# One stage of rounds in place of a norm stage and a latent-projection stage, in a hybrid decoder step

## The chip, the cores and the metric

The kernel runs on one core of a Trainium2 chip. The metric is the device time of one execution, in microseconds (us). The core has five engines that take their instructions in order and hand work to each other by semaphores: PE (TensorE, matrix products and transposes into PSUM), ACT (ScalarE), DVE (VectorE), POOL (GpSimd) and SP (SyncE, which here issues most DMAs).

## The reference, cut to what matters

The reference is one layer of a decoder for a prompt of 2048 tokens and a sample group of 32 tokens (8 x 4). Everything starts with one norm and one wide projection:

```
xn = x * rsqrt(mean(x*x) + 1e-6) * g_pre                       # 2048 x 1024 and 32 x 1024
[qa | ka | va | za | cq | ckv | kpe | zb | ma | mb] = xn @ w_in
```

The change touches the norm and the columns cq (256), ckv (128) and kpe (32), 416 in all, the latents of the second attention branch:

```
cq_n  = rms_norm(cq, g_q)            # feeds the queries later on
ckv_n = rms_norm(ckv, g_kv)          # an output, and keys and values later on
kpe_r = kpe * cos + rot(kpe) * sin   # an output, and a key shared by all heads
```

All other columns, the attention branches, the gates and the output projection are worked out in later stages, which the change leaves as they are. Everything is float32; products are made from a high and a low part of each operand, three matmuls in place of one.

## The kernel before, in words

`run_stages` calls one stage after the other; a stage is one block of engine programs, and the next block begins when all engines and the stage's awaited stores are through. The first two stages are the subject.

`stage_norm` goes over 17 tiles (16 of 128 prompt tokens, one of 32 sample tokens), two at a time, in a loop over pairs (`peeled`). For a tile, SP loads 128 x 1024 of x (L160); ACT takes the sum of squares (L173) and a square root (L176); DVE inverts it (L200) and multiplies x by it and by the gains (L203); PE transposes the result in eight blocks of 128 x 128 into PSUM (L229); ACT copies that into `xT_hi` (L181), rounded to the matmul's format; DVE writes the rest into `xT_lo` (L208). `xT_hi` and `xT_lo` stay in SBUF for all later projections. Both tiles of a pair go through one step before ACT and DVE turn to the next step.

`stage_latents` first loads the 416 columns of `w_in` in eight chunks through two buffers (L276), with ACT making the high part (L306) and DVE the low part (L342); PE waits for all eight (`w_lo`). Then it goes over the same 17 tiles: PE makes 24 matmuls (8 chunks of the 1024 x 3 parts; L109, L110, L111 in `split_matmul`) into one of four PSUM banks; ACT takes two sums of squares, a copy and two roots (L323 to L331); DVE finishes the latents in `nat` (L350 to L364); SP stores ckv and kpe (L291, L292); PE transposes the tile's latents in four pieces (L376, L378), one tile later; ACT lays these out in `cqT`, `ckvT`, `kpeT` (L314 to L316), which hold all 2080 tokens. When the last tile is laid out, SP stores the three whole (L295 to L297) and waits for them.

The third stage, `stage_dilated`, begins with loads of its own weights (its tiles are named `dil_...`).

Of the kernel before, what the change touches and what calls it, by code (L numbers as in the profile page):

```python
# [26 lines left out]
F32 = mybir.dt.float32  # L27
# [5 lines left out]
ds = bass.ds  # L33
# [99 lines left out]


def stage_norm(nc, t, xT, xs, ident):

    with ExitStack() as ctx:
        m = Mem(nc, ctx, "norm")
        xin = [m.sb(f"xin{b}", [P, D]) for b in range(2)]
        xn = [m.sb(f"xn{b}", [P, D]) for b in range(2)]  # L140
        junk = m.sb("junk", [P, D])
        g = m.sb("g_rows", [P, D])
        eps = m.sb("eps", [P, 1])
        stat = [m.sb(f"stat{b}", [P, 4]) for b in range(2)]
        tp = [m.ps(f"tp{b}", [P, KC, P]) for b in range(2)]
        consts = m.sem("consts")
        x_in = [m.sem(f"x_in{b}") for b in range(2)]
        eps_set, squared, rooted, inverted = (m.sem(n) for n in ("eps_set", "squared", "rooted", "inverted"))
        xn_ready, tp_ready, hi_ready, lo_ready = (m.sem(n) for n in ("xn_ready", "tp_ready", "hi_ready", "lo_ready"))

        with nc.Block() as block:
            @block.sync
            def _(sp):
                sp.dma_start(ident[:, :], t["ident"]).then_inc(consts, 16)
                sp.dma_start(g[:, :], t["g_pre"].partition_broadcast(P)).then_inc(consts, 16)

                def load(i):
                    for b in range(2):
                        waits(sp, xn_ready, i + b - 1)
                        sp.dma_start(xin[b][:, :], t["x_prompt"][ds((i + b) * P, P), :]).then_inc(x_in[b], 16)  # L160

                peeled(sp, NT // 2, 2, load)
                sp.wait_ge(xn_ready, NT - 1)
                sp.dma_start(xin[0][0:NS, :], t["x_sample"]).then_inc(x_in[0], 16)

            @block.scalar
            def _(act):
                act.wait_ge(eps_set, 1)

                def square(n, b, loads, rows):  # L170
                    act.wait_ge(x_in[b], loads)
                    waits(act, inverted, n - 1)
                    act.activation(junk[0:rows, :], xin[b][0:rows, :], ACT.Square,  # L173
                                   accum_out=stat[b][0:rows, 0:1]).then_inc(squared, 1)
                    act.wait_ge(squared, n + 1)
                    act.activation(stat[b][0:rows, 1:2], stat[b][0:rows, 0:1], ACT.Sqrt, bias=eps[0:rows, :],  # L176
                                   scale=1.0 / D).then_inc(rooted, 1)

                def high(n, b, out, rows):
                    act.wait_ge(tp_ready, n + 1)  # L180
                    act.activation(out, tp[b][:, :, 0:rows], ACT.Copy).then_inc(hi_ready, 1)  # L181

                def pair(i):
                    for b in range(2):
                        square(i + b, b, i * 8 + 16, P)
                    for b in range(2):
                        high(i + b, b, xT[0][:, :, ds((i + b) * P, P)], P)

                peeled(act, NT // 2, 2, pair)
                square(NT, 0, NT * 8 + 16, NS)  # L190
                high(NT, 0, xs[0][:, :, :], NS)

            @block.vector
            def _(dve):
                dve.memset(eps[:, :], EPS).then_inc(eps_set, 1)
                dve.wait_ge(consts, 32)

                def norm(n, b, rows):
                    dve.wait_ge(rooted, n + 1)
                    dve.reciprocal(stat[b][0:rows, 2:3], stat[b][0:rows, 1:2]).then_inc(inverted, 1)  # L200
                    dve.wait_ge(inverted, n + 1)
                    waits(dve, tp_ready, n - 1)
                    dve.scalar_tensor_tensor(xn[b][0:rows, :], xin[b][0:rows, :], stat[b][0:rows, 2:3],  # L203
                                             g[0:rows, :], ALU.mult, ALU.mult).then_inc(xn_ready, 1)

                def low(n, b, hi, lo, rows):
                    dve.wait_ge(hi_ready, n + 1)
                    dve.tensor_tensor(lo, tp[b][:, :, 0:rows], hi.bitcast(F32), ALU.subtract).then_inc(lo_ready, 1)  # L208

                def pair(i):  # L210
                    for b in range(2):
                        norm(i + b, b, P)
                    for b in range(2):
                        at = ds((i + b) * P, P)
                        low(i + b, b, xT[0][:, :, at], xT[1][:, :, at], P)

                peeled(dve, NT // 2, 2, pair)
                norm(NT, 0, NS)
                low(NT, 0, xs[0][:, :, :], xs[1][:, :, :], NS)

            @block.tensor
            def _(pe):
                pe.wait_ge(consts, 32)

                def turn(n, b, rows):
                    pe.wait_ge(xn_ready, n + 1)
                    waits(pe, lo_ready, n - 1)
                    for c in range(KC):
                        last = pe.transpose(tp[b][:, c, 0:rows], xn[b][0:rows, c * P:(c + 1) * P],  # L229
                                            ident[0:rows, 0:rows])  # L230
                    last.then_inc(tp_ready, 1)

                def pair(i):
                    for b in range(2):
                        turn(i + b, b, P)

                peeled(pe, NT // 2, 2, pair)
                turn(NT, 0, NS)


def stage_latents(nc, t, xT, xs, ident):

    with ExitStack() as ctx:
        m = Mem(nc, ctx, "lat")
        raw = [m.sb(f"raw{b}", [P, LAT]) for b in range(2)]
        w = [m.sb(f"w_{h}", [P, KC, LAT], F32R) for h in ("hi", "lo")]
        lat = [m.sb(f"lat{b}", [P, LAT]) for b in range(2)]
        nat = [m.sb(f"nat{b}", [P, LAT]) for b in range(2)]
        rot = [m.sb(f"rot{b}", [P, 2 * ROPE]) for b in range(2)]
        junk_q, junk_kv = m.sb("junk_q", [P, QL]), m.sb("junk_kv", [P, KL])  # L250
        stat = [m.sb(f"stat{b}", [P, 6]) for b in range(2)]
        eps = m.sb("eps", [P, 1])
        gkv = m.sb("gkv_rows", [P, KL])
        gq = m.sb("gq_cols", [P, QL // P])
        cs = m.sb("rope_rows", [P, NT + 1, 2, ROPE])
        cqT = m.sb("cqT", [P, QL // P, TOK])
        ckvT = m.sb("ckvT", [P, TOK])
        kpeT = m.sb("kpeT", [ROPE, TOK])
        pj = [m.ps(f"pj{b}", [P, 512]) for b in range(4)]
# [2134 lines left out]
```

## Time and profile before

| | us |
|---|---|
| timed, median of 3 runs (3608.48 to 3610.82) | 3609.86 |
| the profiled execution's own time | 3615.65 |
| span of that execution, first to last instruction | 3614.1 |
| PE busy in the span | 3344.3 (93%) |
| DVE, ACT, POOL busy | 1314.3, 954.7, 443.8 |
| mean granted TensorE clock, share of full speed | 0.954 |

The span is divided by the profile into 40 slices of some 90 us; the two stages of the change fill the first two and a little of the third. A line of the timeline reads: start, duration, engine, line of the kernel, operation, what it writes <- what it reads, shapes, count, and in brackets how long the engine sat idle before it and what released it. SPq is SP's queue of DMA issues, PEld the weight loads of PE. A transpose is listed as MATMUL.

### The profile page before, as it was taken

The numbers are of one execution on the slowest core, as the hardware profiler recorded it, in microseconds if no ns is written. First come the engines' busy times: TensorE is split into PE (matmuls) and PEld (weight loads), VectorE is DVE, ScalarE is ACT, GpSimd is POOL, SyncE is SP. The second block draws the span as 40 slices with busy tenths as digits, with TensorE's granted clock in tenths as the row PEclk, the third lists the DMA queues.
The fourth block names the chain that finished last, engine by engine and source line by source line (L and its number), as shares of the span: only waits on it lengthen the run. The fifth ranks groups of instructions, "written<-read, shape, count | busy, mean of one in ns | idle before, by whom it ended". The sixth has DMA issues, their size and how long they took to land. (4 is left out here: it accounts for less than half of the span.)

```text
span 3614.1 us, 51439 instructions
## 1 busy us (share of the span) xinstructions
PE 3344.3 (93%) x19384; PEld 2785.8 (77%) x19384; DVE 1314.3 (36%) x3518; ACT 954.7 (26%) x1839; POOL 443.8 (12%) x599
## 2 busy tenths in 40 slices
PE   3979999999999999899999997899999999488799
PEld 3968888888788887799999996566666667288787
DVE  5202222222222222222111112466555666388433
ACT  5412222222222222122222222233333334110121
POOL 0000000000000000000000002223322312044200
PEclk6989999999999998899999999899999999699899
DMA  3143333333323332332222214133333223377343
GB/s 115 27 165 120 122 121 100 108 111 97 120 92 106 96 103 72 98 95 82 84 84 84 82 60 138 56 106 116 116 116 108 75 59 114 128 253 245 104 139 119
DMA packets 348182, 391.52 MB, mean 108 GB/s; under 512 B 111465, under 2 KB 305738, under 8 KB 345898
## 3 DMA queue, kind: packets, MB, share of 16 engines
q1 hardware_dynamic: 308474, 173.53, 17.5%
q0 software_dynamic: 39472, 214.82, 17.1%
q8 instruction: 150, 2.46, 0.3%
q14 instruction: 86, 0.70, 0.1%
HBM read 309.62 MB, written 166.67 MB: 132 GB/s over the span
## 5 line engine op out<-in xcount | busy, mean ns | idle before, releaser
L109 PE MATMUL dil_PJ<-all_xT_hi,dil_w_hi 128*128 128x512 f32 x1152 | 469.6, 408 | 17.6 <-DVE dil_w_lo L634 17.6
L111 PE MATMUL dil_PJ<-all_xT_hi,dil_w_lo 128*128 128x512 f32 x1152 | 454.7, 395 | 0.0
L110 PE MATMUL dil_PJ<-all_xT_lo,dil_w_hi 128*128 128x512 f32 x1152 | 454.6, 395 | 0.0
L109 PE MATMUL gate_ps<-all_xT_hi,gate_w_hi 128*128 128x416 f32 x960 | 346.1, 360 | 13.5 <-DVE gate_w_lo L1082 13.5
L111 PE MATMUL gate_ps<-all_xT_hi,gate_w_lo 128*128 128x416 f32 x960 | 337.7, 352 | 0.0
L110 PE MATMUL gate_ps<-all_xT_lo,gate_w_hi 128*128 128x416 f32 x960 | 337.0, 351 | 0.0
L1857 PE MATMUL mla_S<-mla_k,mla_q 96*128 96x512 f32 (+3 forms) x640 | 294.2, 578 | 12.7 <-ACT mla_p L1645 7.3
L109 PEld LDWEIGHTS dil_PJ<-all_xT_hi,dil_w_hi 128*128 128x128 f32 x1152 | 216.9, 188 | 98.9 <-issue 36.1
L1885 PE MATMUL mla_O<-mla_v,mla_pT 128*128 128x66 f32 x2176 | 272.8, 275 | 4.6 <-DVE mla_rec L1804 4.6
L1885 PEld LDWEIGHTS mla_O<-mla_v,mla_pT 128*128 128x128 f32 x2176 | 265.1, 196 | 9.0 <-issue 7.2
L111 PEld LDWEIGHTS dil_PJ<-all_xT_hi,dil_w_lo 128*128 128x128 f32 x1152 | 216.7, 188 | 50.1
L110 PEld LDWEIGHTS dil_PJ<-all_xT_lo,dil_w_hi 128*128 128x128 f32 x1152 | 217.1, 188 | 43.5
L668 DVE COPY dil_rec<-dil_O 128x256 f32<-128x256 f32 x96 | 40.8, 425 | 510.9 <-PE dil_O L791 510.9
L1789 DVE TENSOR_REDUCE mla_stat<-mla_S 128x1 f32<-128x1024 f32 (+2 forms) x192 | 175.0, 912 | 85.2 <-PE mla_S L1857 80.7
L579 ACT ACTIVATE dil_sm<-dil_sm,dil_neg 128x256 f32<-128x256 f32 (+1 forms) x384 | 146.1, 451 | 222.9 <-DVE dil_neg L655 222.9
L1645 ACT ACTIVATE mla_p<-mla_S,mla_stat 128x1024 f32<-128x1024 f32 (+2 forms) x192 | 166.1, 865 | 129.9 <-DVE mla_stat L1791 128.9
L648 DVE CUSTOM_DVE_ANT_0 dil_sm<-dil_S,dil_bias 128x256 f32<-128x256 f32 (+1 forms) x384 | 117.6, 362 | 215.9 <-PE dil_S L763 213.2
L109 PEld LDWEIGHTS gate_ps<-all_xT_hi,gate_w_hi 128*128 128x128 f32 x960 | 180.7, 188 | 18.7 <-DVE gate_w_lo L1082 13.7
L1857 PEld LDWEIGHTS mla_S<-mla_k,mla_q 96*128 96x128 f32 x640 | 111.9, 200 | 107.2 <-issue 79.6
L1653 ACT ACTIVATE mla_pT<-mla_T 128x512 f32<-128x512 f32 (+1 forms) x192 | 104.0, 542 | 325.0 <-PE mla_T L1867 324.1
L110 PEld LDWEIGHTS gate_ps<-all_xT_lo,gate_w_hi 128*128 128x128 f32 x960 | 181.4, 189 | 1.9
L111 PEld LDWEIGHTS gate_ps<-all_xT_hi,gate_w_lo 128*128 128x128 f32 x960 | 180.7, 188 | 2.4
(272 smaller groups left out, 5743.1 us busy)
## 6 DMA issues: line engine op xcount, KB each, us to landing
out_win_sample<-in_state_win POOLq DMA_DIRECT2D x16, 4088.0 KB, 15.2
mla_kv<-in_state_win POOLq DMA_DIRECT2D x72, 512.0 KB, 12.5
scr_gates<-gate_out POOLq DMA_DIRECT2D x120, 208.0 KB, 2.3
mla_qb<-scr_hs POOLq DMA_DIRECT2D x32, 768.0 KB, 12.2
dil_raw<-in_w_in SPq DMA_DIRECT2D x36, 512.0 KB, 4.3
gate_ckv<-in_cache_ckv SPq DMA_DIRECT2D x256, 64.0 KB, 1.8
out_win_sample<-in_state_win POOLq DMA_DIRECT2D x8, 2032.0 KB, 8.6
jp_gm<-scr_gates SPq DMA_DIRECT2D x56, 256.0 KB, 4.8
```

The costliest lines, as they stand in the source:

```text
L109: pe.matmul(out, w[0], x[0], start=first, stop=False)
L110: pe.matmul(out, w[0], x[1], start=False, stop=False)
L111: return pe.matmul(out, w[1], x[0], start=False, stop=last)
L579: last = act.activation(part, part, ACT.Exp, bias=neg[u % 2][:, s, h:h + 1])
L648: last = dve.tensor_tensor_reduce(sm[:, s, h, 0:nk * P], S[:, h, s * 2 * P:(s * 2 + nk) * P], bias[:, h, (2 - nk) * P:2 * P], 1.0, LOWEST, ...
L668: dve.tensor_copy(rec[u % 4][:, :, 0:2 * HD], O[:, :, 2:2 + 2 * HD])
L1645: act.activation(p[u % 2][:, 0:nk * P], s2[:, 0:nk * P], ACT.Exp, bias=stat[u % 2][:, 1:2], scale=B_SCALE).then_inc(exped, 1)
L1653: act.activation(pT[u % 2][0][:, 0:q, :], T[:, 0, 0:q, :], ACT.Copy).then_inc(t_out_a, 1)
L1789: dve.tensor_reduce(stat[b2][:, 0:1], s2[:, 0:nk * P], AX.X, ALU.max).then_inc(maxed, 1)
L1857: last = pe.matmul(S[:, 2 * (u % 2) + a // 4, 0:width], q96[0:NOPE + ROPE, i * P:(i + 1) * P], k96[0:NOPE + ROPE, (j + a) * P:(j + a) * P ...
L1885: last = pe.matmul(O[:, u % 2, 0:VB], pT[u % 2][k // 4][:, k % 4, :], v[:, j + k, :], start=k == 0, stop=k == nk - 1)
```

## The change: one stage, in rounds

`stage_norm` and `stage_latents` are taken out, and `stage_norm_and_latents` does both. It runs 21 rounds with no loop instruction; round i squares and normalises tile i, turns it (PE), makes the high part and the low part and the projection of tile i-1, takes the projected latents of tile i-2, transposes the latents of tile i-3 and lays out those of tile i-4. The weights are loaded and split inside round 0. The projection has two PSUM banks in place of four (`pj`), since the turned x keeps four (`xp`). `cqT`, `ckvT` and `kpeT` hold one tile each, twice, and each tile of them is stored on its own.

```diff
+def stage_norm_and_latents(nc, t, xT, xs, ident):
...
+        cqT = [m.sb(f"cqT{b}", [P, QL // P, P]) for b in range(2)]
+        ckvT = [m.sb(f"ckvT{b}", [P, P]) for b in range(2)]
+        kpeT = [m.sb(f"kpeT{b}", [ROPE, P]) for b in range(2)]
+        xp = [m.ps(f"xp{b}", [P, KC, P]) for b in range(2)]
+        pj = [m.ps(f"pj{b}", [P, 512]) for b in range(2)]
+        tp = [m.ps(f"tp{b}", [P, 4, P]) for b in range(2)]
...
+        TILES = NT + 1
+        ROUNDS = TILES + 4
...
+                def load_x(i):
+                    if i > 1:
+                        sp.wait_ge(xn_ready, i - 1)
...
+                def load_weights(c):
+                    if c > 1:
+                        sp.wait_ge(w_lo, c - 1)
+                    sp.dma_start(raw[c % 2][:, :], t["w_in"][c * P:(c + 1) * P, C_CQ:C_CQ + LAT]).then_inc(w_in[c % 2], 16)
+
+                load_x(0)
+                sp.dma_start(ident[:, :], t["ident"]).then_inc(x_consts, 16)
+                sp.dma_start(g[:, :], t["g_pre"].partition_broadcast(P)).then_inc(x_consts, 16)
+                load_x(1)
+                load_weights(0)
+                load_weights(1)
+                sp.dma_start(gkv[:, :], t["g_kv"].partition_broadcast(P)).then_inc(consts, 16)
...
+                def store_turned(i):
+                    sp.wait_ge(turned, i + 1)
+                    cols = slice(0, rows_of(i))
+                    sp.dma_start(t["cqT"][:, :, at(i)].rearrange("c p n -> p c n"), cqT[i % 2][:, :, cols])\
+                        .then_inc(t_stored[i % 2], 16)
+                    sp.dma_start(t["ckvT"][:, at(i)], ckvT[i % 2][:, cols]).then_inc(t_stored[i % 2], 16)
+                    sp.dma_start(t["kpeT"][:, at(i)], kpeT[i % 2][:, cols]).then_inc(t_stored[i % 2], 16)
...
+                for i in range(ROUNDS):
+                    if i + 2 < TILES:
+                        load_x(i + 2)
+                    if i == 0:
+                        for c in range(2, KC):
+                            load_weights(c)
+                    if 0 <= i - 2 < TILES:
+                        store_latents(i - 2)
+                    if 0 <= i - 4 < TILES:
+                        store_turned(i - 4)
...
+                def lay_out(i):
+                    b, n = i % 2, rows_of(i)
+                    act.wait_ge(tp_ready, i + 1)
+                    if i > 1:
+                        act.wait_ge(t_stored[b], 48 * (i // 2))
...
+                for i in range(ROUNDS):
+                    if i < TILES:
+                        square(i)
+                    if 0 <= i - 1 < TILES:
+                        high(i - 1)
+                    if i == 0:
+                        for c in range(KC):
+                            high_weight(c)
+                        act.wait_ge(consts, 64)
+                    if 0 <= i - 2 < TILES:
+                        take(i - 2)
+                    if 0 <= i - 4 < TILES:
+                        lay_out(i - 4)
...
+                for i in range(ROUNDS):
+                    if i < TILES:
+                        norm(i)
+                    if 0 <= i - 1 < TILES:
+                        low(i - 1)
+                    if i == 0:
+                        for c in range(KC):
+                            low_weight(c)
+                        dve.wait_ge(consts, 64)
+                    if 0 <= i - 2 < TILES:
+                        finish(i - 2)
...
+                def project(i):
+                    pe.wait_ge(lo_ready, i + 1)
+                    if i == 0:
+                        pe.wait_ge(w_lo, KC)
+                    if i > 1:
+                        pe.wait_ge(copied, i - 1)
+                        pe.wait_ge(squared, 2 * (i - 1))
...
+                for i in range(ROUNDS):
+                    if i < TILES:
+                        turn_x(i)
+                    if 0 <= i - 1 < TILES:
+                        project(i - 1)
+                    if 0 <= i - 3 < TILES:
+                        turn_latents(i - 3)
...
-        stage_norm(nc, t, xT, xs, ident)
-        stage_latents(nc, t, xT, xs, ident)
+        stage_norm_and_latents(nc, t, xT, xs, ident)
```

The functions `square`, `high`, `high_weight`, `take`, `lay_out` (ACT), `norm`, `low`, `low_weight`, `finish` (DVE), `turn_x`, `project`, `turn_latents` (PE) issue the same compute instructions, on tiles of the same sizes, as the lines of before that the section on the kernel names.

PE, between one projection and the next. Before, in `stage_latents` (`lat_pj` is the projection, `lat_tp` the transposed latents):

```order
L111 MATMUL lat_pj<-lat_w_hi,all_xT_lo 128x416
L376 MATMUL lat_tp<-all_ident,lat_nat 128x128 x3
L378 MATMUL lat_tp<-all_ident,lat_nat 32x128
L109 MATMUL lat_pj<-lat_w_hi,all_xT_hi 128x416
L110 MATMUL lat_pj<-lat_w_lo,all_xT_hi 128x416
```

PE at the same place in a middle round of the change (`nl_xp` is the turned x):

```order
L111 MATMUL nl_pj<-nl_w_hi,all_xT_lo 128x416
L2268 MATMUL nl_tp<-all_ident,nl_nat 128x128 x3
L2269 MATMUL nl_tp<-all_ident,nl_nat 32x128
L2245 MATMUL nl_xp<-all_ident,nl_xn 128x128 x8
L109 MATMUL nl_pj<-nl_w_hi,all_xT_hi 128x416
L110 MATMUL nl_pj<-nl_w_lo,all_xT_hi 128x416
```

Between two projections there now stand the eight transposes of a later tile of x, which before were in the first stage.

ACT, one tile of `stage_latents` before:

```order
L323 ACTIVATE lat_junk_q,lat_stat<-lat_pj 128x256
L325 ACTIVATE lat_junk_kv,lat_stat<-lat_pj 128x128
L327 ACTIVATE lat_lat<-lat_pj 128x416
L329 ACTIVATE lat_stat<-lat_stat,lat_eps 128x1
L331 ACTIVATE lat_stat<-lat_stat,lat_eps 128x1
L314 ACTIVATE lat_cqT<-lat_tp,lat_gq_cols 128x128 x2
L315 ACTIVATE lat_ckvT<-lat_tp 128x128
L316 ACTIVATE lat_kpeT<-lat_tp 32x128
```

ACT, one middle round of the change (`nl_xin` is x as loaded, `nl_xstat` its statistics):

```order
L2123 ACTIVATE nl_junk,nl_xstat<-nl_xin 128x1024
L2125 ACTIVATE nl_xstat<-nl_xstat,nl_eps 128x1
L2131 ACTIVATE all_xT_hi<-nl_xp 128x8x128
L2142 ACTIVATE nl_junk,nl_stat<-nl_pj 128x256
L2143 ACTIVATE nl_junk,nl_stat<-nl_pj 128x128
L2145 ACTIVATE nl_lat<-nl_pj 128x416
L2147 ACTIVATE nl_stat<-nl_stat,nl_eps 128x1
L2149 ACTIVATE nl_stat<-nl_stat,nl_eps 128x1
L2158 ACTIVATE nl_cqT<-nl_tp,nl_gq_cols 128x128 x2
L2159 ACTIVATE nl_ckvT<-nl_tp 128x128
L2160 ACTIVATE nl_kpeT<-nl_tp 32x128
```

Three instructions of the first stage now come ahead of the second stage's eight in each round, and the copy into `xT_hi` stands between a root and a projected tile.

SP's queue at the end of the stage before:

```order
L291 DMA out_ckv_sample<-lat_nat 32x128
L292 DMA out_kpe_sample<-lat_nat 32x32
L295 DMA scr_cqT<-lat_cqT 128x2080 x2
L296 DMA scr_ckvT<-lat_ckvT 128x2080
L297 DMA scr_kpeT<-lat_kpeT 32x2080
```

SP's queue at the end of the new stage:

```order
L2088 DMA out_ckv_sample<-nl_nat 32x128
L2089 DMA out_kpe_sample<-nl_nat 32x32
L2094 DMA scr_cqT<-nl_cqT 128x2x128
L2096 DMA scr_ckvT<-nl_ckvT 128x128
L2097 DMA scr_kpeT<-nl_kpeT 32x128
L2094 DMA scr_cqT<-nl_cqT 128x2x128
L2096 DMA scr_ckvT<-nl_ckvT 128x128
L2097 DMA scr_kpeT<-nl_kpeT 32x128
L2094 DMA scr_cqT<-nl_cqT 128x2x32
L2096 DMA scr_ckvT<-nl_ckvT 128x32
L2097 DMA scr_kpeT<-nl_kpeT 32x32
```

The four whole stores have become three small ones for each tile; the stores of the last three turned tiles stand behind those of the last latents.

## Rows read from the trace of the kernel before

**Rows 1.** Busy time by stretch: PE, PEld, DVE, ACT, POOL, granted clock, DMA share, GB/s
```profile
12.50:79.00 66.50, 30.40 (x136) 27.12 (x136) 43.80 (x50) 38.02 (x65) 0.00 (x0) 0.67 0.37 112
...
102.00:170.00 68.00, 68.00 (x385) 66.73 (x384) 14.73 (x98) 31.34 (x150) 0.00 (x0) 1.00 0.07 18
...
21.60:25.30 3.70, 3.67 (x16) 3.28 (x16) 1.68 (x2) 1.02 (x1) 0.00 (x0) 1.00 0.60 178
```

**Rows 2.** Timeline of the kernel's start
```profile
1.00 0.40 SPq L154 DMA_DIRECT2D all_ident<-in_ident  x1
...
8.01 1.28 ACT L173 ACT_TABLE_LOAD   x1 [8.01 <-DMA norm_xin<-in_x_prompt]
...
12.37 1.28 DVE L203 SCALAR_TENSOR_TENSOR norm_xn<-norm_xin,norm_stat,norm_g_rows 128x1024 f32<-128x1024 f32 x1
```

**Rows 3.** Timeline of one pair of tiles in the norm stage
```profile
26.35 1.05 ACT L173 ACTIVATE norm_junk<-norm_xin 128x1024 f32<-128x1024 f32 x1
...
27.52 0.29 ACT L176 ACTIVATE norm_stat<-norm_stat,norm_eps 128x1 f32<-128x1 f32 x1
...
27.85 0.16 DVE L200 RECIPROCAL norm_stat<-norm_stat 128x1 f32<-128x1 f32 x1
28.13 1.28 DVE L203 SCALAR_TENSOR_TENSOR norm_xn<-norm_xin,norm_stat,norm_g_rows 128x1024 f32<-128x1024 f32 x1
...
29.55 3.67 PE L229 MATMUL norm_tp<-all_ident,norm_xn 128*128 128x128 f32 x16 [4.25 <-DVE norm_xn L203]
...
31.65 1.02 ACT L181 ACTIVATE all_xT_hi<-norm_tp 128x1024 f32 x1 [2.47 <-PE norm_tp L229]
32.82 1.22 DVE L208 TENSOR_TENSOR all_xT_lo<-norm_tp,all_xT_hi 128x1024 f32 x1 [2.01 <-ACT all_xT_hi L181]
```

**Rows 4.** Timeline of the weights, to the first projection
```profile
81.52 1.09 ACT L306 ACTIVATE lat_w_hi<-lat_raw 128x416 fp32r<-128x416 f32 x2 [3.15 <-DMA lat_raw<-in_w_in]
82.10 1.13 DVE L342 TENSOR_TENSOR lat_w_lo<-lat_raw,lat_w_hi 128x416 fp32r<-128x416 f32 x2 [2.87 <-ACT lat_w_hi L306]
...
94.67 0.71 PE L109 MATMUL lat_pj<-lat_w_hi,all_xT_hi 128*128 128x416 f32 x1 [16.73 <-DVE lat_w_lo L342]
```

**Rows 5.** Timeline of PE where its matmuls become shorter
```profile
99.69 0.55 PE L111 MATMUL lat_pj<-lat_w_hi,all_xT_lo 128*128 128x416 f32 x1
100.04 0.52 PE L109 MATMUL lat_pj<-lat_w_hi,all_xT_hi 128*128 128x416 f32 x1
```

**Rows 6.** Timeline of one latent tile: PE, then ACT, then DVE
```profile
106.44 0.49 PE L376 MATMUL lat_tp<-all_ident,lat_nat 128*128 128x128 f32 x3
...
106.79 0.43 PE L109 MATMUL lat_pj<-lat_w_hi,all_xT_hi 128*128 128x416 f32 x1
...
111.39 0.49 PE L376 MATMUL lat_tp<-all_ident,lat_nat 128*128 128x128 f32 x3
...
111.59 0.38 ACT L323 ACTIVATE lat_junk_q<-lat_pj 128x256 f32<-128x256 f32 x1 [2.66 <-PE lat_pj L111]
...
112.98 0.63 ACT L314 ACTIVATE lat_cqT<-lat_tp,lat_gq_cols 128x128 f32<-128x128 f32 x2
...
113.64 0.25 ACT L316 ACTIVATE lat_kpeT<-lat_tp 32x128 f32<-32x128 f32 x1
...
114.00 0.18 DVE L364 TENSOR_TENSOR lat_nat<-lat_rot 128x32 f32<-128x32 f32 x1
```

**Rows 7.** Timeline of the latent stage's end and the next stage's first instruction
```profile
180.92 0.37 ACT L323 ACTIVATE lat_junk_q<-lat_pj 32x256 f32<-32x256 f32 x1 [2.64 <-PE lat_pj L111]
...
184.59 0.82 SPq L295 DMA_DIRECT2D scr_cqT<-lat_cqT  x2
...
195.05 0.13 POOL L542 MEMSET dil_v<- 128x16 f32 x1 [194.35 <-POOLq L271]
```

**Rows 8.** DMA issues of the two stages: count, KB each, median us to landing
```profile
norm_xin<-in_x_prompt SPq DMA_DIRECT2D x16, 512.0 KB, 4.2
...
scr_ckvT<-lat_ckvT SPq DMA_DIRECT2D x1, 1040.0 KB, 8.1
...
out_kpe_sample<-lat_nat SPq DMA_DIRECT2D x1, 4.0 KB, 1.6
```

More of the change, by code:

```diff
@@ L132, in peeled @@
         body(i * step)
[L135 to L238, printed above, removed]
```

299 lines of the change are left out of this document (158 added, 141 removed).

## The prediction

> **What bounds the kernel now.** I read the busy time by stretch first, then the timeline of each stretch. Only the kernel's first 195 us are touched, and there no engine is full until the projections run. In the norm stage, 66.5 us hold 30.4 us of PE, 43.8 of DVE and 38.0 of ACT [rows 1]: three engines take turns, since within a pair PE waits for the normalised tiles (4.25 us idle before its 16 transposes), ACT for PE, DVE for ACT [rows 3]. Then comes a stretch with nothing but weights: PE's first projection starts at 94.67 and has waited 16.73 us for the last remainder [rows 4]. From 102 to 170 PE is busy all the time at a granted clock of 1.00, with ACT under half and DVE under a quarter busy [rows 1]: that stage is bound by PE. At its end the last tile is taken at 180.92, SP begins the four large stores at 184.59, and the next stage's first instruction is at 195.05 [rows 7]; the stores alone cost 10.5 us with every engine idle.
>
> So the first two stages are worth 195.05 us, of which PE needs 17 times 4.95 [rows 6], 84, for the projections. The question is how far a round is from PE's own work.
>
> **The change part by part.**
>
> *A round on PE.* One latent tile takes 4.95 us from transposes to transposes (106.44 to 111.39): 0.35 for the four pieces, 4.60 for 24 matmuls, a pitch of 0.19 [rows 6]. The round adds eight transposes. Sixteen took 3.67 in the norm stage, 0.23 each [rows 3]; the same shape inside the projections takes about 0.11 (three full pieces and one narrow one in 0.35) [rows 6]. The first is the pace at the clock's lower level, 1.2 GHz, the second at 2.4. PE works without a pause in the rounds, as from 102 to 170, so I take 0.11: 0.9 us. A round is 0.9 + 4.95 = 5.85, with one more switch of shape 5.9. The other end is 0.23, 1.84 us for eight and 6.8 a round.
>
> *Does the rest of the round fit under it?* ACT: square and root 1.46 (26.35 to 27.81), high part 1.02 [rows 3], take 1.39 (111.59 to 112.98), lay out 0.91 (to 113.89) [rows 6]: 4.8. DVE: inverse and product 1.56 (27.85 to 29.41), low part 1.22 [rows 3], finishing at most 1.20 (112.98 to 114.18) [rows 6]: 4.0. Both are under 5.9, but what counts is the chain through them. After a projection ends, ACT takes it (1.39), lays out an older tile (0.91), squares a new one (1.46); DVE normalises that (1.56) and then makes the low part that the next projection but one waits for (1.22): 6.54, and five hand-overs of 0.04 (root to inverse, 27.81 to 27.85) to 0.15 (high to low, 32.67 to 32.82) [rows 3], 6.7 to 7.3. PE meanwhile has 0.35 + 0.9 + 4.6 + 0.35 + 0.9 = 7.1. So the chain just fits; at the slow end it costs 0.2 in every second round, 2 us in all. I take nothing. The high part (1.02) runs beside DVE's 1.56.
>
> *Memory traffic in a round.* The x load is issued when a tile is normalised and is needed two rounds less 3 us later, 8.7 us; it lands in 4.2 [rows 8]. The three turned stores wait on SP behind two latents stores, and `lay_out` waits for those of two tiles before: cover 11.8 - 0.9, need three issues of 0.41 [rows 7] and a landing between 1.6 and 8.1 [rows 8], 9.3 at worst. Cost nothing; without that cover a late landing would hold ACT and through it every projection. SP is free for 48 more issues.
>
> *The start.* x comes first in SP's queue, not third: landed at 1.00 + 4.2 = 5.2 in place of 8.01 [rows 2, 8]. Tile 0 was normalised 5.64 after its landing (8.01 to 13.65, with a table load at its head) [rows 2], now at 10.85. By then the first two weight chunks, two issues behind the second x tile, should have landed, but DVE's first remainder stands behind that product. From first remainder to first projection took 12.57 (82.10 to 94.67) [rows 4], four pairs each waiting for the one before; the change keeps two buffers, so the weights are split at 23.4, and 0.5 later as an x tile and the rope rows queue ahead: 23.9 (bounds: 22 if x lands at once, 27 if it lands at 8.01 as before). ACT, 0.6 earlier, squares tile 1 to 24.8; DVE normalises to 26.3, makes the low part of tile 0 to 27.7; PE turns tile 1 from 26.4 at the lower clock (1.84) and projects tile 0 from 28.2. Before, that was 94.67.
>
> *The rounds.* Before, PE ran at the long pitch of 0.35 from 94.67 to 100.04 [rows 4, 5], 5.4 us after a long idle; here from 26.4 to 31.8. Ten matmuls at 0.35 and 14 at 0.19 end projection 0 at 34.5. Projections 1 and 2 have no latents to turn: 5.5 each, 45.5. Thirteen rounds of 5.9: 122.2. The last has no x to turn: 4.95, 127.2.
>
> *The tail.* From take to finished latents 2.6 (111.59 to 114.18) [rows 6]: 129.8. SP issues two stores, then only the three of tile 14, 0.41 each: the last is issued at 131.4 and lands 1.6 later [rows 8], 133.0; ACT's lay-out of tile 16 waits for them, 0.91, 133.9; three more issues and a landing: 136.4. Small stores stand between 1.6 and the 8.1 of the 1040 KB store [rows 8]; the new ones are 128 KB at most, so 1.6, and two landings at 8.1 would add 13.
>
> *Sum.* The next stage starts at 136.4 in place of 195.05: 58.6, I take 58. Everything behind it moves up as it is. The profiled span of 3614.1 becomes 3556. That execution took 3615.65 in all, the timed median is 3609.86, so the timed kernel comes to 3609.86 - 58 = 3552.
>
> **The rivals.**
>
> *Forecast: PE-bound rounds.* 3552, own range 3546 to 3560: start 2 us earlier or 3 later, hand-overs 2, tail to half its bound. Chance 0.69.
>
> *The chain bounds the rounds.* It fits by 0.4 us at the fast hand-over only. If queued work or late semaphores make it 8.5, two rounds take 1.4 more, a round is 6.6 and thirteen of them cost 9: 3561. For it: the slack is small. Against it: in unrolled code the hand-overs are 0.04. Chance 0.15.
>
> *The transposes are slow at either clock.* From 21.60 to 25.30 the granted clock reads 1.00 while 16 transposes still take 3.67 [rows 1]. If that reading is right, 0.23 is their price whatever the clock, rounds are 6.8, and fifteen of them cost 14: 3566. Against: the same duration in the pair of rows 3, which belongs to a stretch of mean clock 0.67 that must hold lower readings, and 0.11 in rows 6 for the same shape. Chance 0.08.
>
> *The clock swings.* PE now waits for another engine at three places in each round, and `pj` has two banks in place of four. If its clock fell in each round to the mean 0.67 of the norm stage [rows 1], a round is 5.9 / 0.67 = 8.8 and sixteen cost 46: 3598, still faster by 0.3%. Against: the norm stage had PE idle more than half of the time, the rounds have waits of tenths of a microsecond. Chance 0.05. The Trainium skill, in "TensorE: Matmul & The Clock Gate", section "A second HAM failure mode: psum-queue depth-cycling", speaks for this rival: a kernel that cycled through PSUM banks paused briefly between groups often enough for its clock to go back and forth. By that rule the time would be this rival's, by the stretch from 102 to 170, where `pj` cycles too and the clock stays at 1.00, it would be the forecast; no row yet shows two banks.
>
> *The other side: PE stays at the lower clock through the whole stage.* Matmuls at 0.35 and transposes at 0.23 make a round 8.4 + 1.84 + 0.7 = 10.9, five more, sixteen times 80: 3632, slower by 0.6%. It decides from a round of 5.9 + 58/16 = 9.5 on. Against: at that pace PE has no waits at all, and without waits the clock rose within 5.4 us [rows 4, 5]. Chance 0.03.
>
> **How the numbers follow.** About 0.2%, 7 us, is what a measurement can tell from no change. Forecast, chain, transposes and swinging clock are all faster by more: 0.69 + 0.15 + 0.08 + 0.05 = 0.97, of which I move 0.01 to no change for a swing somewhat deeper than the norm stage's; slower 0.03. The range reaches from the forecast's lower end to beyond the slow transposes with a start 3 us late and a slow hand-over: 3546 to 3572, which leaves out the two clock cases and a little of the others, 1 to 2 in 10.
>
> **What would show it.** In the changed profile: the first projection at about 28 and the 17th ending at about 127; a pitch of 5.9 between transposes of x, PE without idle time and a clock of 1.00 from about 32 on; eight transposes in 0.9; `lay_out` of the last tile released by a store, and the next stage's first instruction near 136. Wrong would be: PE idle before `turn_x` released by DVE in most rounds (chain), eight transposes in 1.8 at full clock, a clock below 1.00 in the rounds, or ACT released by `scr_cqT` stores before the tail.

## The result, and the profile after

| | change, us | before, us | ratio, 95% interval |
|---|---|---|---|
| first timing, median (lowest to highest, runs) | 3556.16 (3547.63 to 3559.12, 4) | 3609.17 (3601.70 to 3610.82, 4) | 0.9850, 0.9834 to 0.9866 |
| second timing | 3551.50 (3547.66 to 3557.50, 5) | 3605.77 (3602.07 to 3618.02, 9) | 0.9844, 0.9824 to 0.9864 |
| profiled execution: span | 3556.7 | 3614.1 | |
| first instruction of the next stage | 136.55 | 195.05 [rows 7] | |

The kernel became 53.0 and 54.3 us faster; the forecast said 58 and 3552. The two stages themselves gave up 195.05 - 136.55 = 58.5 us. The profile after, place by place, against the rows ahead of the prediction:

The timeline of the start (columns as before: start, duration, engine, line, operation, and in brackets the idle time and its releaser) answers to [rows 2, 4, 5]:

```profile
4.78 1.28 ACT L2123 ACT_TABLE_LOAD   x1 [4.78 <-DMA nl_xin<-in_x_prompt]
...
9.14 1.28 DVE L2189 SCALAR_TENSOR_TENSOR nl_xn<-nl_xin,nl_xstat,nl_g_rows 128x1024 f32<-128x1024 f32 x1
...
22.36 1.06 ACT L2135 ACTIVATE nl_w_hi<-nl_raw 128x416 fp32r<-128x416 f32 x2 [2.62 <-DMA nl_raw<-in_w_in]
22.94 1.10 DVE L2199 TENSOR_TENSOR nl_w_lo<-nl_raw,nl_w_hi 128x416 fp32r<-128x416 f32 x2 [2.58 <-ACT nl_w_hi L2135]
...
26.43 1.97 PE L2245 MATMUL nl_xp<-all_ident,nl_xn 128*128 128x128 f32 x8 [13.92 <-DVE nl_xn L2189]
...
28.05 0.69 PE L109 MATMUL nl_pj<-nl_w_hi,all_xT_hi 128*128 128x416 f32 x1
...
28.54 0.55 PE L110 MATMUL nl_pj<-nl_w_lo,all_xT_hi 128*128 128x416 f32 x1
...
28.89 0.55 PE L111 MATMUL nl_pj<-nl_w_hi,all_xT_lo 128*128 128x416 f32 x1
...
32.33 0.35 PE L109 MATMUL nl_pj<-nl_w_hi,all_xT_hi 128*128 128x416 f32 x1
...
32.52 0.35 PE L110 MATMUL nl_pj<-nl_w_lo,all_xT_hi 128*128 128x416 f32 x1
```

x is there at 4.78, tile 0 is normalised at 10.42, the weights are split at 24.04, the first projection starts at 28.05, where before it was 94.67. The weights still come in pairs that ACT waits for, 2.62 us at the last, and PE sits idle for 13.92 us. From start to start the projection's matmuls first stand 0.35 us apart (28.54, 28.89) and from 32.33 on 0.19.

A middle round, on the timeline, answers to [rows 6]:

```profile
63.61 1.04 PE L2245 MATMUL nl_xp<-all_ident,nl_xn 128*128 128x128 f32 x8
64.40 0.44 PE L109 MATMUL nl_pj<-nl_w_hi,all_xT_hi 128*128 128x416 f32 x1
...
69.06 0.49 PE L2268 MATMUL nl_tp<-all_ident,nl_nat 128*128 128x128 f32 x3
...
69.26 0.39 ACT L2142 ACTIVATE nl_junk<-nl_pj 128x256 f32<-128x256 f32 x1 [1.31 <-PE nl_pj L111]
...
69.49 1.04 PE L2245 MATMUL nl_xp<-all_ident,nl_xn 128*128 128x128 f32 x8
...
74.35 1.22 DVE L2195 TENSOR_TENSOR all_xT_lo<-nl_xp,all_xT_hi 128x1024 fp32r<-128x1024 f32 x1
...
76.17 0.44 PE L109 MATMUL nl_pj<-nl_w_hi,all_xT_hi 128*128 128x416 f32 x1
```

From transposes to transposes it is 69.49 - 63.61 = 5.88 us. Eight transposes hold PE for 64.40 - 63.61 = 0.79 to the start of the next matmul, and the 24 matmuls behind them take 69.06 - 64.40 = 4.66, 0.19 each. ACT waits 1.31 us for PE's projection: PE is the engine that sets the pace. The low part made from tile to tile ends at 74.35 + 1.22 = 75.57, and the projection that reads it starts at 76.17, so 0.60 us of slack are left in that chain.

Busy time in the rounds (columns as in [rows 1]), then the longest of the waits in the rounds, 60 to 120 (engine, line <- releaser: us in total, times, longest):

```profile
60.00:125.00 65.00, 65.00 (x396) 62.34 (x395) 37.88 (x109) 47.79 (x162) 0.00 (x0) 1.00 0.36 110
```

```profile
ACT nl_junk L2142 <- PE nl_pj L111: 13.1, 10, 1.3
```

PE is busy in all of the 65 us at a granted clock of 1.00, the upper level of 2.4 GHz; it waits for nobody, ACT waits for it once in each of ten rounds, and no wait of PE, ACT or DVE is ended by a DMA.

The end of the stage, on the timeline, answers to [rows 7]:

```profile
126.90 0.49 PE L2268 MATMUL nl_tp<-all_ident,nl_nat 128*128 128x128 f32 x3
...
129.48 0.17 DVE L2220 TENSOR_TENSOR nl_nat<-nl_rot 32x32 f32<-32x32 f32 x1
...
131.50 0.44 SPq L2097 DMA_DIRECT2D scr_kpeT<-nl_kpeT  x1
...
133.08 0.47 ACT L2158 ACTIVATE nl_cqT<-nl_tp,nl_gq_cols 128x32 f32<-128x32 f32 x2 [2.88 <-DMA scr_kpeT<-nl_kpeT]
...
134.64 0.43 SPq L2097 DMA_DIRECT2D scr_kpeT<-nl_kpeT  x1
136.55 0.13 POOL L284 MEMSET dil_v<- 128x16 f32 x1 [135.85 <-POOLq L2056]
```

The last lay-out waits 2.88 us for a store that SP issued at 131.50, and that lands 1.6 later; 1.9 us after the last issue, at 134.64, the next stage starts. From the end of the last projection, where the transposes of 126.90 start, to the next stage it is 136.55 - 126.90 = 9.65 us.

**Why 53 and 54 and not 58.5.** Behind the first instruction of the next stage, the program is the same. From there to the end of the span, eleven profiled executions (before, the change twice, eight experiments) took 3409.9 to 3420.2 us: 3614.1 - 195.05 = 3419.1 before, 3556.7 - 136.55 = 3420.2 and 3549.6 - 136.98 = 3412.6 in two executions of the change. One and the same kernel differs there by 7.6 us.

The first instruction of POOL in the stage of the second attention branch, late in that rest, parts it in two. Its line before, then in the change:

```profile
2216.39 0.44 POOL L1581 MEMSET mla_spz<- 128x416 f32 x1 [5.15 <-POOLq L2299]
```

```profile
2160.61 0.44 POOL L1323 MEMSET mla_spz<- 128x416 f32 x1 [5.09 <-POOLq L2313]
```

The change's other execution has it at 2161.10, so 55.8 and 55.3 of the 58.5 are left there. The way from the next stage's first instruction to it takes 2021.3 us before, 2024.1 in both executions of the change and 2020.7 to 2024.7 in the experiments; whether the 2.8 given back belong to the change stays open at that spread. From there to the end the eleven executions take 1387.7 to 1397.7, and this last part holds most of their differences: of the change's two executions, the longer has 1396.1 there at a mean granted clock over the span of 0.962, the shorter 1388.5 at 0.964. Why it differs is open. The experiments below are therefore read by the end of the stage, where the change's two executions agree to 0.43 us, and not by the whole time.

### The profile page after: what moved, and what is told of

Same layout as the page of the kernel before. It is cut to its first block and busy times, and to the rows that moved or that the text cites. A ratio compares the mean times of both kernels' runs of the same rounds, so it can differ in the third digit from the quotient of the medians.

```text
span 3556.7 us, 51335 instructions
## 1 busy us (share of the span) xinstructions
PE 3331.7 (94%) x19384; PEld 2776.4 (78%) x19384; DVE 1312.5 (37%) x3517; ACT 952.7 (27%) x1839; POOL 444.0 (12%) x599
## 3 DMA queue, kind: packets, MB, share of 16 engines
q0 software_dynamic: 39472, 214.82, 17.4%
```

## The experiments

Each line says where the next stage's first instruction came; before it is 195.05, in the change 136.55. The first six were timed in one execution each (3607.59, 3587.85, 3558.70, 3589.84, 3552.81 and 3549.20 us, in their order here), the last two in five.

**1. Only the stores, in the old order.** The kernel before, with the turned latents stored tile by tile.

```diff
-        cqT = m.sb("cqT", [P, QL // P, TOK])
+        cqT = [m.sb(f"cqT{b}", [P, QL // P, P]) for b in range(2)]
...
-                for c in range(QL // P):
-                    sp.dma_start(t["cqT"][c], cqT[:, c, :]).then_inc(stored, 16)
...
+                    if i:
+                        store_turned(i - 1, P)
+                store_turned(NT, NS)
...
+                    waits(act, t_stored[b], 48 * (i // 2))
```

> The kernel before with one part of the change alone: the turned latents are kept one tile at a time in two buffers and stored tile by tile; the two stages stay. Theory (the large stores at the end are a cost of their own, and the tail of the change is SP's queue plus a landing): the next stage's first instruction comes some 9.4 us after the last projection ends, as in the change, in place of 14: at about 190 in place of 195.05, so this part is worth 4 to 5 us of the 58.5. Rival (the stores were waiting for memory bandwidth or in the queue, and small rows are dearer): 195 or later, and the four-store tail was no loss.

Its timeline from the end of the last projection, where the first transposes behind it start; ahead of it the line at the same place of the kernel before:

```profile
180.72 0.49 PE L376 MATMUL lat_tp<-all_ident,lat_nat 128*128 128x128 f32 x3
```

```profile
179.77 0.49 PE L385 MATMUL lat_tp<-all_ident,lat_nat 128*128 128x128 f32 x3
...
187.75 0.13 POOL L551 MEMSET dil_v<- 128x16 f32 x1 [187.05 <-POOLq L272]
```

187.75, 7.3 us earlier than before and earlier than expected; one execution took 3607.59 us beside 3604.95 of the kernel before, which says nothing against it at the spread above. Not all of the 7.3 comes from the stores: the last projection ends 0.95 earlier as well, at 179.77 in place of 180.72, and the first already starts 0.49 earlier, at 94.18, before there is a tile to store. From there to the next stage it is 7.98 us in place of 195.05 - 180.72 = 14.33, so the small stores are worth 6.35 here. In the change this stretch takes 9.65, since its last lay-out waits for a store, so there they give 4.7.

**2. The change with its rounds undone.** One new stage, loads and stores as in the change, but all tiles are normalised and turned before the first is projected.

```diff
                 for i in range(ROUNDS):
                     if i < TILES:
                         turn_x(i)
+                for i in range(1, ROUNDS):
                     if 0 <= i - 1 < TILES:
                         project(i - 1)
```

(The programs of SP, ACT and DVE are split in the same way, with their second loop from round 2 on.)

> The changed stage with its rounds undone: same instructions, buffers, weights and stores, but every engine first goes through all tiles of the norm (one tile after the other, weights split behind the first) and then through all tiles of the projection. Theory (most of the gain is PE projecting while ACT and DVE normalise): the norm phase takes 2.9 a tile on DVE and ends near 70, projections take 17 times 4.95 and 2.7 for the lower clock, the next stage starts at 162 to 170, some 30 us later than the change's 136.55; the rest of the gain, 25 to 33, is then the weights, the unpaired norm and the stores. Rival (the gain comes from the weights and the single stage, and overlap is worth little): within 10 us of 136.55.

Busy time in its norm phase, then its timeline:

```profile
10.00:75.00 65.00, 31.12 (x128) 25.08 (x128) 44.24 (x56) 41.70 (x71) 0.00 (x0) 1.00 0.46 141
```

```profile
47.09 1.97 PE L2248 MATMUL nl_xp<-all_ident,nl_xn 128*128 128x128 f32 x8 [1.88 <-DVE nl_xn L2191]
...
77.25 0.71 PE L109 MATMUL nl_pj<-nl_w_hi,all_xT_hi 128*128 128x416 f32 x1
...
163.22 0.49 PE L2271 MATMUL nl_tp<-all_ident,nl_nat 128*128 128x128 f32 x3
...
172.85 0.13 POOL L284 MEMSET dil_v<- 128x16 f32 x1 [172.15 <-POOLq L2056]
```

172.85: without the rounds 36.3 us of the 58.5 are gone. That is the overlap itself. It is more than the 30 or so expected, because the norm phase alone runs at some 3.3 us a tile and not 2.9: ACT waits some 0.5 for an x tile in most tiles (0.56 before the square at 46.99), and PE is busy for less than half of the time.

The rows also part the other 22.2 us. The first projection starts at 77.25 in place of 94.67 [rows 4], 17.4 earlier; 16.7 of this is the time for which PE waited for the weights to be loaded and split [rows 4], and here it goes straight on from its last transposes. The projections take 163.22 - 77.25 = 85.97, before 180.72 - 94.67 = 86.05. The rest is the tail, 9.63 in place of 14.33, 4.7 less. So the 58.5 are 36.3 of overlap, 17.4 ahead of the first projection, nearly all of it the weights, and 4.7 behind the last.

The busy time and the line at 47.09 settle the rival of the slow transposes. The granted clock reads 1.00 over the stretch in which eight transposes take 1.97 us; in the change's rounds it reads 1.00 too, and eight take 1.04. One price cannot hold at both, so the reading of this early stretch, as that of [rows 1], is not the level at which PE worked there. The matmuls say the same: in the change the reading is 1.00 from the start, and at it they stand 0.35 apart at 28.54 and 0.19 at 32.33. By the Trainium skill, "TensorE: Matmul & The Clock Gate", section "Part 4: PE-mode transpose", the full clock does not engage for transposes. The rounds do not bear that out, since eight take 1.04 there, at the pace of the upper level. A norm phase of nothing but transposes at the long duration agrees with it, but PE idles for half of that phase as well, and no run here separates the two.

**3 and 4. More work on ACT.** One, then three more squares of the same tile in each round, ahead of the one that counts.

```diff
+                    for n in range(1):
+                        act.activation(junk[r, :], xin[b][r, :], ACT.Square).then_inc(more, 1)
+                        act.wait_ge(more, i * 1 + n + 1)
```

> The change with one more square of the x tile on ACT ahead of the real one in each round (1.05 us, with its wait some 1.2); its output is thrown away. Theory (PE bounds the rounds, with about 0.6 us of slack in the chain through ACT and DVE over two rounds, as the low part ends 0.59 before its projection starts in the changed profile): the pitch between transposes of x rises from 5.89 to about 6.2, and PE waits a few tenths before projections. Rival 1 (ACT idles 1.3 a round, which covers it): pitch stays 5.89 to 5.95. Rival 2 (the chain already bounds): 6.5.

> The change with three more squares of the x tile in each round, about 3.6 us; their output is thrown away. ACT then has some 8.3 us of work a round, PE 5.9. Theory (short waits leave the clock alone): the pitch is 8.2 to 8.6, PE idles some 2.5 in each, the granted clock stays at 1.00 and the eight transposes take 0.9. Rival (waits between groups of matmuls make the clock go back and forth): granted clock in the rounds clearly under 1.00, matmuls at a pitch of 0.35 in part of the rounds, and a pitch of 9 to 11.

Waits of the kernel with one more square, 60 to 120, then its timeline:

```profile
PEld nl_xp L2249 <- DVE nl_xn L2193: 1.6, 5, 0.3
PEld nl_pj L109 <- DVE all_xT_lo L2199: 1.4, 5, 0.3
```

```profile
60.06 1.04 PE L2249 MATMUL nl_xp<-all_ident,nl_xn 128*128 128x128 f32 x8
...
72.40 1.04 PE L2249 MATMUL nl_xp<-all_ident,nl_xn 128*128 128x128 f32 x8
```

Three more squares, busy time, timeline and, last, busy time behind it:

```profile
60.00:80.00 20.00, 15.90 (x93) 14.03 (x92) 10.62 (x30) 19.71 (x52) 0.00 (x0) 1.00 0.35 96
```

```profile
70.14 1.09 PE L2249 MATMUL nl_xp<-all_ident,nl_xn 128*128 128x128 f32 x8 [1.33 <-DVE nl_xn L2193]
...
77.88 1.09 PE L2249 MATMUL nl_xp<-all_ident,nl_xn 128*128 128x128 f32 x8 [1.32 <-DVE nl_xn L2193]
...
147.50 0.68 PE L2249 MATMUL nl_xp<-all_ident,nl_xn 32*128 32x32 f32 x8 [1.31 <-DVE nl_xn L2193]
...
148.64 0.46 PE L109 MATMUL nl_pj<-nl_w_hi,all_xT_hi 128*128 128x416 f32 x1 [0.45 <-DVE all_xT_lo L2199]
```

```profile
149.50:152.00 2.50, 2.50 (x9) 2.38 (x8) 0.37 (x2) 0.00 (x0) 0.00 (x0) 0.50 0.34 96
```

With one more square the transposes of x start at 60.06, 66.15 and 72.40, 6.17 us apart on average, as expected: 0.28 of its price of 1.08 (a third of the 3.23 that three of them take on ACT) shows. The chain runs over two rounds, so its slack of 0.60 leaves 0.48 to be paid per two rounds, 0.24 per round. PE now waits for DVE in every second round, 0.3 us at each of two places, which is the sign named for the chain rival, though that asked for most rounds. The stage ends at 141.78. With three more the pitch is 77.88 - 70.14 = 7.74 and ACT is busy for 19.71 of 20 us: ACT is the bound. The expected pitch was above that, because it added ACT's instructions at their full durations; the records of neighbours on one engine overlap, and ACT's work in a round of the change is 47.79 / 65 x 5.89 = 4.33 us, not the 4.8 of the prediction. The stage ends at 169.47.

From 60 to 149 the clock stays at 1.00 and the matmuls 0.19 apart, although PE waits some 1.3 us before its transposes in every round. Then it falls. In the round that turns the last, narrow tile, PE waits 1.31 us, is through its eight short transposes in 0.68, and waits 0.45 more; from 149.2 to 152.4 the reading is 0.50, the lower level, and the matmuls stand 0.35 apart. So a part of what the rival said did come, once, though not a pitch of 9 to 11 in every round.

**5. One bank for the projection.**

```diff
-        pj = [m.ps(f"pj{b}", [P, 512]) for b in range(2)]
+        pj = [m.ps(f"pj{b}", [P, 512]) for b in range(1)]
...
-                    if i > 1:
-                        pe.wait_ge(copied, i - 1)
-                        pe.wait_ge(squared, 2 * (i - 1))
+                    if i:
+                        pe.wait_ge(copied, i)
+                        pe.wait_ge(squared, 2 * i)
```

> The change with one PSUM bank for the projection in place of two, so that every projection waits until ACT has copied the one before. Theory (between two projections PE has the two sets of transposes, 1.2 us, and ACT's copy ends about 1.3 after the projection): the pitch rises by 0.1 to 0.3 from 5.89, the clock stays at 1.00, the stage ends 2 to 5 us later. Rival (cycling through banks with short waits makes the clock swing, and two banks only just avoid it): granted clock under 0.95 in the rounds and a stage 20 us longer or more.

```profile
58.81 1.04 PE L2245 MATMUL nl_xp<-all_ident,nl_xn 128*128 128x128 f32 x8
...
64.91 1.04 PE L2245 MATMUL nl_xp<-all_ident,nl_xn 128*128 128x128 f32 x8
```

```profile
60.00:125.00 65.00, 64.77 (x383) 61.59 (x383) 37.83 (x108) 46.66 (x156) 0.00 (x0) 1.00 0.39 112
```

First its timeline, then its busy time in the rounds. The clock is 1.00, and the matmuls of a projection are still 0.19 apart; the pitch is 64.91 - 58.81 = 6.10, since the copy out of the bank has to end before the next projection's first matmul, and the stage ends at 140.97, 4.4 later than in the change. What the Trainium skill tells of a kernel that cycled through PSUM banks and whose clock went back and forth ("TensorE: Matmul & The Clock Gate", section "A second HAM failure mode: psum-queue depth-cycling"), which the prediction named for this rival, did not come here with two banks or with one: PE is busy for 64.77 of the 65 us. With the waits of experiment 4 the clock held through the rounds of full tiles, and fell once behind them.

**6. Six buffers for the raw weights in place of two.**

```diff
+        RB = 6
-        raw = [m.sb(f"raw{b}", [P, LAT]) for b in range(2)]
+        raw = [m.sb(f"raw{b}", [P, LAT]) for b in range(RB)]
...
-                    if c > 1:
-                        sp.wait_ge(w_lo, c - 1)
+                    if c >= RB:
+                        sp.wait_ge(w_lo, c - RB + 1)
```

> The change with six buffers for the raw weight chunks in place of two, the first six loads issued at once. Theory (the start of the change is still bound by weight pairs that wait for the pair before, three waits of some 2.6 to 3.6 us on ACT): the first projection moves from 28.05 to 18 to 21, and the next stage's first instruction from 136.55 to 127 to 130. Rival (the loads are bound by memory traffic at the start, with x, gains and rope rows in the queue): the first projection stays later than 25.

```profile
8.34 4.81 SPq L2082 DMA_DIRECT2D nl_rope_rows<-in_rope_rows  x1
...
13.66 0.90 SPq L2069 DMA_DIRECT2D nl_raw<-in_w_in  x2
...
17.58 1.04 ACT L2136 ACTIVATE nl_w_hi<-nl_raw 128x416 fp32r<-128x416 f32 x2 [3.94 <-DMA nl_raw<-in_w_in]
...
23.25 0.70 PE L109 MATMUL nl_pj<-nl_w_hi,all_xT_hi 128*128 128x416 f32 x1
```

The timeline of its start: the first projection comes at 23.25, 4.8 earlier than in the change and later than expected, and the stage ends at 131.15, 5.4 earlier and also later than expected. Six chunks are split in one go, but the last two wait for SP, whose queue stands from 8.34 to 13.15 at the second load of rope rows, the one behind the load of many short rows.

**7. The latents' transposes ahead of the projection as well.** As 6, with `turn_latents(i - 3)` before `project(i - 1)` on PE, and the lay-out and the turned stores a round earlier:

```diff
-                    if 0 <= i - 4 < TILES:
-                        lay_out(i - 4)
+                    if 0 <= i - 3 < TILES:
+                        lay_out(i - 3)
```

> The change with six raw weight buffers, and with the latents' transposes ahead of the projection in each round and laid out and stored one round earlier (four tiles under way in place of five). Theory (start bound by weight pairs, tail by SP's queue behind the last latents): first projection at 18 to 21, pitch unchanged at 5.89, the tail 1 to 2 us shorter, the next stage's first instruction at 125 to 129, 8 to 11 us faster than the change and 66 to 70 faster than before. Rival (the earlier transposes wait for the latents or the lay-out waits for PE, so the chain bounds the rounds): pitch over 6.1, and 3 us or more of the start's gain lost again.

```profile
122.76 0.49 PE L2269 MATMUL nl_tp<-all_ident,nl_nat 128*128 128x128 f32 x3
...
126.00 0.46 ACT L2159 ACTIVATE nl_cqT<-nl_tp,nl_gq_cols 128x32 f32<-128x32 f32 x2 [0.75 <-PE nl_tp L2270]
...
130.73 0.13 POOL L284 MEMSET dil_v<- 128x16 f32 x1 [130.03 <-POOLq L2057]
```

The last lay-out (its timeline) no longer waits for a store but for PE, and from the end of the last projection to the next stage it is 7.97 us, as in experiment 1, in place of 9.65. The stage's end moved by 0.42 only, less than expected: of the 1.68 saved in the tail, 0.61 goes into a later first projection, at 23.86, and 0.64 into the way from there to the end of the last, 98.90 us against 98.26 in 6. The two executions of the change differ by 0.5 on that way (98.85 and 98.35), so it is no sign that the new order costs anything. Timed: 3546.65 us (3543.90 to 3552.53, 5 runs) against 3605.77, ratio 0.9829 (0.9810 to 0.9849).

**8. The rope rows behind the weights.** As 7, with the two loads of rope rows issued after all eight chunks, and ACT and DVE waiting for the constants in round 2 in place of round 0.

```diff
-                sp.dma_start(cs[:, 0:NT, :, :], t["rope_rows"][0:SEQ].rearrange("(i p) s r -> p i s r", p=P))\
-                    .then_inc(consts, 16)
...
                         for c in range(RB, KC):
                             load_weights(c)
+                        sp.dma_start(cs[:, 0:NT, :, :], t["rope_rows"][0:SEQ].rearrange("(i p) s r -> p i s r", p=P))\
+                            .then_inc(consts, 16)
...
+                    if i == 2:
                         act.wait_ge(consts, 64)
```

> Six weight buffers and the latents' transposes ahead of the projection, as in the kernel before it, and the two loads of the rope rows (many short rows; the issue behind the large one lasts 4.81 us in SP's queue with six buffers, 4.60 in the change) moved behind all eight weight chunks, with ACT and DVE waiting for them in round 2. Theory A: with six buffers the first projection came at 23.25 and not 18 to 21 because SP's queue stood at the second rope load from 8.34 to 13.15, so that the third x tile was issued at 13.19 and the last two weight chunks at 13.66, which ACT then waited 3.94 us for. Then these chunks are now issued at 11 to 12.5, are split by 17, the first projection starts at 20.5 to 21.5, and the next stage's first instruction comes at 128 (127.5 to 129) in place of 130.73. Theory B: the early loads share the DMA engines and it is their rate that counts, so that the chunks land at the same time whatever stands ahead: first projection after 23, next stage at 130 to 131.5. The whole kernel differs by less than its executions spread.

```profile
11.04 0.83 SPq L2069 DMA_DIRECT2D nl_raw<-in_w_in  x2
...
12.39 2.76 SPq L2105 DMA_DIRECT2D nl_rope_rows<-in_rope_rows  x1
...
14.83 1.18 ACT L2136 ACTIVATE nl_w_hi<-nl_raw 128x416 fp32r<-128x416 f32 x2 [2.00 <-DMA nl_raw<-in_w_in]
...
20.57 0.69 PE L109 MATMUL nl_pj<-nl_w_hi,all_xT_hi 128*128 128x416 f32 x1
...
127.25 0.13 POOL L284 MEMSET dil_v<- 128x16 f32 x1 [126.55 <-POOLq L2057]
```

The last chunks are issued 2.6 us earlier than in 6, ACT waits 2.00 in place of 3.94, the first projection starts at 20.57 and the next stage at 127.25: theory A, and a little more than it said. From the issue of these chunks to ACT's work on them it is 3.8 us, in 6 3.9: they did not come faster, only sooner. The queue that stood still was the cause; the waits for the constants were not, since in 6 ACT goes on without idle time from the last chunk to the square that stands behind them. Timed: 3542.65 us (3537.39 to 3548.50, 5 runs) against 3605.50 (8 runs), ratio 0.9826 (0.9809 to 0.9844). It has the lowest median of all versions, 8.9 us below the second timing of the change, with 9.3 us less in the stage; over experiment 7 the timing alone can't tell it, and its interval still touches that of the change.

## Why the prediction was right, step by step

| step | predicted | measured |
|---|---|---|
| x landed, tile 0 normalised | 5.2, 10.85 | 4.78, 10.42 |
| weights split, first projection | 23.9, 28.2 | 24.04, 28.05 |
| projections 0 and 2 end | 34.5, 45.5 | 34.62, 45.52 |
| pitch of a round | 5.9 | 5.89 |
| last projection ends, last latents finished | 127.2, 129.8 | 126.90, 129.65 |
| last lay-out, next stage | 133.0, 136.4 | 133.08, 136.55 |
| saved up to the next stage | 58 | 58.5 |

- **What bounds the rounds.** PE, as said: no idle time, ACT waiting for it. The pitch came out because the eight transposes were taken at the pace that the same shape has inside the projections, and not at that of the norm stage. That it came out to 0.01 is in part luck: eight transposes held PE for 0.79 and not 0.9, the latents' four pieces for 69.49 - 69.06 = 0.43 and not 0.35, the matmuls for 4.66 and not 4.60.
- **The chain.** It was sized at 6.7 to 7.3 us against 7.1 of PE. PE has 76.17 - 69.06 = 7.11; the chain, from the end of a projection to the low part, has 75.57 - 69.06 = 6.51. The term was too large, since it added full durations, while a following instruction on ACT or DVE can start before the record of the last one has ended: the low part starts at 74.35, and the product ahead of it on DVE, 1.28 long, started at 73.15. The rival was real but 0.6 us away; one more square of 1.08 us brings it in.
- **Slow transposes, swinging clock, lower clock.** Eight transposes in 1.04, the clock at 1.00 through the rounds with two banks and with one: none of the three happened in the change. The price of the swing, 46 us, was worked out from the mean reading of 0.67 in the norm stage, which was no mean of PE's pace: all full tiles' transposes there last as in [rows 3], at the long duration. The rival itself is not dead: with two waits of 1.31 and 0.45 us in one round, experiment 4 had the clock at 0.50 for 3 us. The change has no such waits in its rounds.
- **The tail.** The wait of the last lay-out for a store was there as forecast, with a landing of 1.6 us. Experiment 7 shows that it need not be: it costs 1.7 us.
- **The start.** The two-buffer weights took as long as forecast (2.6 us of waiting in each of the last two pairs), and six buffers with the loads in a better order take 7.5 us off the first projection.
- **The sum.** 58 us against 53.0 and 54.3 in the medians. "Everything behind it moves up as it is" held to 2.8 us as far as 2161 us, where 55.8 and 55.3 are left; what is missing beyond lies within the 10 us by which the last part differs between single executions. That the second median, 3551.50, falls within 1 us of the forecast is luck at this spread; the forecast of the stage, 136.4 against 136.55, is the better test of it.

## What to carry to other kernels

When two stages follow each other, one with three engines taking turns and one full of PE, price the merged round by PE's work at the pace of the full stage, and then check the longest chain through the other engines against PE's time over as many rounds as the chain spans; a slack of 0.6 us held here for thirteen rounds. Read a change to one stage by where the next stage begins, not by the whole time, when the rest differs by 10 us from one execution to the next. Look down the DMA queue ahead of the first large wait: constants that are needed only in round 2 stood ahead of the weights and, with six buffers, cost 3 us.

## What the runs showed of the hardware that was not expected

- In SP's queue the issue behind the load of 2048 short rope rows lasts 4.60 us in the change, 4.81 in experiment 6, 5.09 in experiment 7, 2.76 in experiment 8 and 1.80 in the kernel before, where nearly all single stores in the rounds last 0.33 to 0.48 to issue. What stands behind it in the queue is issued only when it is through: in experiment 6 it lasts to 8.34 + 4.81 = 13.15, and the next x tile is issued at 13.19.
- The granted clock reads 1.00 at the start of an execution while eight transposes take 1.97 us; later, at the same reading, they take 1.04. The change's matmuls go from 0.35 apart to 0.19 at 32.33 without a change of the reading. At the start, durations tell the level, and the reading doesn't.
- With waits of 1.33 us before the transposes of each round of 7.74 us (experiment 4), PE kept the upper level from 60 to 149 us; in the round with waits of 1.31 and 0.45 us around the short transposes of the last tile it lost it, and had it back 3 us later, at 152.5.
